# One step of a two-layer hybrid decoder on one core: the modulation units of the prelude in another order, and the first norm's last group in two halves

## The reference, cut to what matters

```python
def adaln(c, w, b):
    return jnp.split(jax.nn.silu(c) @ w + b, 6, axis=-1)

def modulate(x, g, shift, scale):
    return rms_norm(x, g) * (1.0 + scale[:, None, :]) + shift[:, None, :]
...
    for layer in range(DEPTH):
        mp = adaln(c_prompt, w_ada[layer], b_ada[layer])
        ...
        hp = modulate(yp, g_mix[layer], mp[0], mp[1])
        ...
            op, st_conv_p, st_gla_p = mix_ab(hp @ w_in_ab, conv0, gla0, ...)
```

## Time and profile before

| | |
|---|---|
| median of 3 runs | 2760.37 us |
| profiled execution, its own time | 2757.93 us |
| span of the profiled execution | 2756.2 us |
| PE busy | 2676.4 us, 97% of the span |
| DVE, ACT, POOL busy | 1426.5 us, 1160.5 us, 95.9 us |
| weights and inputs read | 592.02 MB |
| busy tenths of PE in the first two of 40 slices | 5, 8; 9 in nearly all others |

### The profile page before, as it was taken

One profiled execution on the slowest core, in us unless ns is written; L12 is line 12 of the kernel. 1 busy time (PEld: TensorE's weight loads), 2 busy tenths in 40 slices (PEclk: granted clock), 3 DMA queues, 4 the chain that ended last, 5 costly groups with the idle time before them and its releaser, 6 DMA issues.

```text
span 2756.2 us, 48520 instructions
## 1 busy us (share of the span) xinstructions
PE 2676.4 (97%) x20155; PEld 2473.9 (90%) x20155; DVE 1426.5 (52%) x1983; ACT 1160.5 (42%) x1521; POOL 95.9 (3%) x136
## 2 busy tenths in 40 slices
PE   5899999999999999999999999998999999999998
PEld 1688988888898888989999899898999999999998
DVE  1588967664444333444444556656445444445444
ACT  2433256453433322434443446535444433444433
POOL 1100011100000000000000000001000000000000
PEclk8999999999999999999999999999999999999999
DMA  9977769777777788776465544344544455445453
GB/s 392 370 286 275 288 231 179 295 281 284 272 290 260 292 318 317 281 282 244 160 237 161 163 153 136 110 134 159 168 162 161 147 160 190 158 164 167 143 161 128
DMA packets 110042, 603.61 MB, mean 219 GB/s; under 512 B 24829, under 2 KB 26301, under 8 KB 53578
## 3 DMA queue, kind: packets, MB, share of 16 engines
q1 hardware_dynamic: 109898, 601.56, 62.3%
HBM read 592.02 MB, written 9.49 MB: 218 GB/s over the span
## 4 chain that ended last, share of the span: by engine, by line
PE 91%; DMA 4%; DVE 2%; ACT 2%; issue 1%; SPq 0%; DVEq 0%; ACTq 0%
PE ps L882 27%; PE ps L884 26%; PE ps L883 26%; PE ps L1090 5%; DMA pre_ring<-in_w_ada 3%; DMA aring<-in_w_ada 1%; PE ps L1248 1%; ACT w_hi L1409 1%; PE ps L1249 1%; PE ps L1250 1%; PE ps L1103 1%; DMA raw<-in_w_dn 1%; DVE w_lo L1882 1%; PE ps L1072 0%; PE ps L1058 0%
## 5 line engine op out<-in xcount | busy, mean ns | idle before, releaser
L1882 DVE TENSOR_TENSOR w_lo<-raw,w_hi 128x2048 fp32r<-128x2048 f32 (+2 forms) x410 | 804.5, 1963 | 1024.7 <-ACT w_hi L1409 1024.6
L882 PE MATMUL ps<-act_hi,w_hi 128*128 128x288 f32 x4128 | 1234.1, 299 | 6.5 <-DVE w_lo L1882 4.6
L883 PE MATMUL ps<-act_hi,w_lo 128*128 128x288 f32 x4128 | 1219.7, 295 | 0.0
L884 PE MATMUL ps<-act_lo,w_hi 128*128 128x288 f32 x4128 | 1215.5, 294 | 0.0
L1409 ACT ACTIVATE w_hi<-raw 128x2048 fp32r<-128x2048 f32 (+2 forms) x410 | 673.9, 1644 | 1050.3 <-PE ps L884 1033.2
L882 PEld LDWEIGHTS ps<-act_hi,w_hi 128*128 128x128 f32 x4128 | 775.6, 188 | 58.6 <-issue 55.6
L884 PEld LDWEIGHTS ps<-act_lo,w_hi 128*128 128x128 f32 x4128 | 779.0, 189 | 0.0
L883 PEld LDWEIGHTS ps<-act_hi,w_lo 128*128 128x128 f32 x4128 | 777.1, 188 | 0.0
L882 PE MATMUL ps<-hid_hi,w_hi 128*128 128x288 f32 x1408 | 418.8, 297 | 0.6 <-DVE w_lo L1882 0.6
L883 PE MATMUL ps<-hid_hi,w_lo 128*128 128x288 f32 x1408 | 415.4, 295 | 0.0
L884 PE MATMUL ps<-hid_lo,w_hi 128*128 128x288 f32 x1408 | 414.0, 294 | 0.0
(11 more groups left out here) (339 smaller groups left out, 1757.6 us busy)
## 6 DMA issues: line engine op xcount, KB each, us to landing
raw<-in_w_gu SPq DMA_DIRECT2D x172, 1024.0 KB, 5.2
aring<-in_w_ada SPq DMA_DIRECT2D x166, 1024.0 KB, 6.9
raw<-in_w_dn SPq DMA_DIRECT2D x128, 704.0 KB, 4.1
raw<-in_w_ab SPq DMA_DIRECT2D x40, 1024.0 KB, 6.5
raw<-in_w_out SPq DMA_DIRECT2D x64, 512.0 KB, 4.7
raw<-in_w_cd SPq DMA_DIRECT2D x26, 1024.0 KB, 5.2
pre_ring<-in_w_ada SPq DMA_DIRECT2D x16, 1024.0 KB, 10.1
side<-in_w_ada SPq DMA_DIRECT2D x6, 1024.0 KB, 9.8
```

The source lines that it names most:

```text
L882: pe.matmul(bank, w_hi[:, h, cols], hi[:, kt, :], start=begin, stop=False)
L883: pe.matmul(bank, w_lo[:, h, cols], hi[:, kt, :], start=False, stop=False)
L884: mm = pe.matmul(bank, w_hi[:, h, cols], lo[:, kt, :], start=False, stop=end)
L1882: dve.tensor_tensor(w_lo[:, h, 0:w], raw[:, par, h * KT * P:h * KT * P + w], w_hi[:, h, 0:w].bitcast(F32), ALU.subtract).then_inc(split_do ...
```

## The change

The units are loaded and worked in the order 0, 4, 1, 5, 2, 6, 3, 7, so that shift and scale of a group of four tiles come one behind the other. All eight units are written out; the loops over units 1 to 3 are gone. `stat` comes after the third unit. `w_zr` and step 0's weights are loaded right after the third unit, too. `opening(0)` follows the turn of the fifth unit, `opening(1)` that of the sixth, `opening(2)` that of the seventh. The last group's norm, high part, low part and opening go in two halves of two tiles. No multiplication is added or left out.

```diff
+PRE_ORDER = [0, 4, 1, 5, 2, 6, 3, 7]
...
             def load_pre(u, s):
                 if not first_unit(u):
                     sp.wait_ge(ada_used, unit_no(u) * 4 + (s - 3))
-                rows = t["w_ada"][bass.ds(unit_no(u) * 4 + s, 1)]
-                sp.dma_start(pre_slot(s), rows.rearrange("a p n -> p (a n)")).then_inc(ring_landed[s], 16)
+                sp.dma_start(pre_slot(s), t["w_ada"][PRE_ORDER[unit_no(u)] * 4 + s]).then_inc(ring_landed[s], 16)
...
             sp.dma_start(x[:], t["xT"]).then_inc(x_landed, 16)
-            with sp.Fori(0, 3) as i:
-                for s in range(4):
-                    load_pre((i, 1), s)
-            sp.dma_start(raw[:, 1, 0:KT * P], t["w_zr"].rearrange("a p n -> p (a n)")).then_inc(zr_landed, 16)
-            for u in range(4, PRE):
+            for u in range(1, PRE):
                 for s in range(4):
                     load_pre((None, u), s)
-                if u == 4:
+                if u == 2:
+                    sp.dma_start(raw[:, 1, 0:KT * P], t["w_zr"].rearrange("a p n -> p (a n)")).then_inc(zr_landed, 16)
                     load_step(SEGS[0], 0, 0, 0)
...
-            stat()
-            for u in range(4, PRE):
+            for u in range(PRE):
                 for s in range(4):
                     ada_slot((None, u), s)
                 ada_turn((None, u))
-                if u > 4:
-                    opening(u - 5)
-            opening(3)
+                if u == 2:
+                    stat()
+                if u > 3:
+                    for k0, k1 in ((12, 14), (14, 16)) if u == PRE - 1 else ((4 * u - 16, 4 * u - 12),):
+                        opening(k0, k1)
...
                 for b in range(k1 - k0):
-                    j = k0 + b
+                    j = sets_of(k)[g][0] + b
                     ins = act.activation(tn[:, g % 2, b, 0:NP_TOK], tn[:, g % 2, b, 0:NP_TOK], ACT.Identity,
                                          scale=amod[:, j, 0:1], bias=mods[:, shift + j, 0:1])
+                    if k == 0 and g == 3 and b == 1:
+                        L.link(ins)
+                        act.wait_ge(tn_samples, set_no(k, g) + 1)
+                        act.activation(act_hi[:, k0:k0 + 2, :], tn[:, g % 2, 0:2], ACT.Copy).then_inc(nhi_done, 1)
+                        k0 += 2
...
-            squares_of_x(0)
-            squares_of_x(2)
-            with act.Fori(0, 3) as i:
-                ada_copy((i, 1))
-                squares_of_x(4 * i + 4)
-                squares_of_x(4 * i + 6)
+            for j in range(0, 6, 2):
+                squares_of_x(j)
+            ada_copy((None, 1))
+            for j in range(6, KT, 2):
+                squares_of_x(j)
+            ada_copy((None, 2))
             stat_rstd(D)
...
-            for g in range(4):
-                ada_copy((None, 4 + g))
-                norm_group(0, g)
-                if g == 0:
-                    split(SEGS[0], 0, 0, 0)
-                    split(SEGS[0], 0, 0, 1)
+            norm_group(0, 0)
+            ada_copy((None, 3))
+            split(SEGS[0], 0, 0, 0)
+            split(SEGS[0], 0, 0, 1)
+            norm_group(0, 1)
+            ada_copy((None, 4))
+            ada_copy((None, 5))
+            norm_group(0, 2)
+            ada_copy((None, 6))
+            ada_copy((None, 7))
+            norm_group(0, 3)
...
             for g in range(4):
-                ada_bias((None, 4 + g))
-                dve.wait_ge(ada_biased, 5 + g)
+                for u in (2 * g, 2 * g + 1):
+                    if u >= 3:
+                        ada_bias((None, u))
+                dve.wait_ge(ada_biased, 2 * g + 2)
                 scales(0, 4 * g, 4 * g + 4)
                 samples(0, g)
                 lo(0, g)
+                if g < 2:
+                    scaled(0, g + 2)
                 if g == 0:
                     split_lo(SEGS[0], 0, 0, 0)
                     split_lo(SEGS[0], 0, 0, 1)
-                if g < 2:
-                    scaled(0, g + 2)
```

More of the change, by code:

```diff
@@ L1191, in body, with opening @@
                         double_turn(p // 4)
-            def opening(g):
-                tiles_g = range(4 * g, 4 * g + 4)
+            def opening(k0, k1):
+                tiles_g = range(k0, k1)
                 def gate_half(h):
-                    if g == 0:
+                    if k0 == 0:
                         pe.wait_ge(split_done, h + 1)
@@ L1206, in gate_half @@
                         mm = pe.matmul(bank, w_hi[:, h, cols], act_lo[:, kt, :], start=False, stop=(kt == KT - 1))
-                    if g == 3:
+                    if k1 == KT:
                         mm.then_inc(half_done, 1)
-                pe.wait_ge(act_ready, 4 * g + 4)
+                pe.wait_ge(act_ready, k1)
                 gate_half(0)
-                if g == 0:
+                if k0 == 0:
                     pe.wait_ge(zr_split, 2)
@@ L1345, in _ @@
             pe.wait_ge(ones_set, 4)
-            for s in range(4):
-                ada_slot((None, 0), s)
-            ada_turn((None, 0))
-            with pe.Fori(0, 3) as i:
-                for s in range(4):
-                    ada_slot((i, 1), s)
-                ada_turn((i, 1))
-            stat()
-            for u in range(4, PRE):
+            for u in range(PRE):
                 for s in range(4):
@@ L1671, in norm_group @@
                 act.wait_ge(tn_samples, set_no(k, g) + 1)
-                act.activation(act_hi[:, k0:k1, :], tn[:, g % 2, 0:k1 - k0], ACT.Copy).then_inc(nhi_done, 1)
+                at0 = k0 - sets_of(k)[g][0]
+                act.activation(act_hi[:, k0:k1, :], tn[:, g % 2, at0:at0 + k1 - k0], ACT.Copy).then_inc(nhi_done, 1)
             def gate_terms(h):
@@ L2029, in ada_bias @@
                 dve.wait_ge(ada_cols, unit_no(u) + 1)
-                b = bass.ds(unit_no(u) * 4 + VEC["b_ada"], 4)
-                dve.tensor_tensor(mods[:, bass.ds(unit_no(u) * 4, 4), :],
+                at0 = PRE_ORDER[unit_no(u)] * 4
+                b = slice(at0 + VEC["b_ada"], at0 + VEC["b_ada"] + 4)
+                dve.tensor_tensor(mods[:, at0:at0 + 4, :],
                                   ps[:, SEL_BANK, 0:64].rearrange("p (q s) -> p q s", s=16)[:, :, 0:S9],
@@ L2166, in lo @@
                 k0, k1 = sets_of(k)[g]
-                dve.wait_ge(nhi_done, set_no(k, g) + 1)
-                js = slice(k0, k1)
-                dve.tensor_tensor(act_lo[:, js, :], tn[:, g % 2, 0:k1 - k0], act_hi[:, js, :].bitcast(F32), ALU.subtract) \
-                    .then_inc(act_ready, k1 - k0)
+                parts = [(k0, k0 + 2), (k0 + 2, k1)] if k == 0 and g == 3 else [(k0, k1)]
+                for n, (a0, a1) in enumerate(parts):
+                    dve.wait_ge(nhi_done, set_no(k, g) + 1 + n + (k > 0))
+                    js = slice(a0, a1)
+                    dve.tensor_tensor(act_lo[:, js, :], tn[:, g % 2, a0 - k0:a1 - k0], act_hi[:, js, :].bitcast(F32),
+                                      ALU.subtract).then_inc(act_ready, a1 - a0)
             def norm(k, final=False):
@@ L2487, in _ @@
                 dve.tensor_copy(sel2[rows, S9 * r:S9 * r + S9], sel[rows]).then_inc(sel2_ready, 1)
-            ada_bias((None, 0))
-            with dve.Fori(0, 3) as i:
-                ada_bias((i, 1))
+            for u in range(3):
+                ada_bias((None, u))
             for h in range(2):
```

2 lines of the change are left out of this document (1 added, 1 removed).

## The result

The changed kernel took 2766.2 us, the median of 8 runs (2765.3 to 2769.87), beside 2762.1 us for the kernel before (8 runs, 2759.13 to 2763.48). The medians are 4.1 us apart. The ratio on record is 1.0021, its 95% interval 1.0011 to 1.0031: slower by 0.2%, some 5.8 us by the ratio. The median lies above the range that was forecast.

The account below looks back on a forecast made before the run. PE was taken to bound the kernel, so only step 1's first matmul could move. Plus 0.2 us up to the eighth copy and minus 0.6 for the halves gave -0.4: 2757.5 us, 2760.0 on the median; range 2757.0 to 2765.0.

Parts of the forecast that it names:

- Bounds and the first part: PE bounds the kernel; early loads and squares are hidden by the stream; fifth unit's copy waits for split and group 1.
- The opening 4.95: Length in us forecast for `opening(0)` behind the fifth unit, taken from the kernel before's profile.
- Where `opening(0)` falls: Step placing `opening(0)` at 73.8 to 78.7 us, next load at 79.8, a dry spell of 2.8, seventh unit's end at 92.4.
- Of the 2.48 only 0.3 is left: Behind `opening(1)`, the eighth unit's load, issued 2.4 us early, loses 0.3 us of stream; bounds nothing and 2.48.
- Minus 0.6 us: Tail: halving the last group brings step 1's high part to 8.4 us behind the eighth unit's copy, from 9.02.
- the clock: Rival: PE runs `opening(0)`, perhaps also the last opening's halves, at 1.2 GHz, ending slower; chance 0.20.
- both places: Clock rival at `opening(0)` and the last opening's halves together: 2768.2 us; chance 0.05 of the 0.20.
- the first place: Clock rival at `opening(0)` alone: 2764.9 us at half the clock, 2762.5 if half of it is slow.
- Two dry spells: Rival: `opening(1)` also costs the load stream its full 2.48 us, 2.2 more than forecast: 2762.2 us; chance 0.08.
- Sum: Whole kernel: 0.2 - 0.6 = -0.4 us, 2757.5 for an execution like the profiled one, 2760.0 on the median; chance 0.60.

Follow-up runs that it names:

- `after_again`: The changed kernel, unaltered, run and profiled a second time; ratio to the kernel before 1.0019.
- `both_places`: The changed kernel plus matmuls with unread results behind slots of the fifth and seventh units, ahead of the last group's first half and behind its second; ratio 0.9999.
- `last_place`: The changed kernel plus matmuls with unread results only at the tail: six ahead of the last group's first half, three behind its second; ratio 1.0018.
- `w_all`: The changed kernel plus unread matmuls: two behind each fifth-unit slot, six ahead of the last group's first half, three behind its second; ratio 1.0012.
- `before_again`: The kernel before, unaltered, run and profiled a second time; ratio to its first measurement 0.9994.
- `spread`: The changed kernel with openings 0 to 2 in three pieces of 12 matmuls, behind the first three slots of the sixth to eighth units; ratio 1.0020.
- `unblocked`: The changed kernel with the split of step 0's weights ahead of group 0's norm on ACT and DVE; ratio to the kernel before 1.0005.

## Why the prediction was wrong

**Bounds and the first part: right.** The fifth unit's last slot starts at 70.01 (forecast 69.9), its copy at 71.85 (72.2), `opening(0)` at 73.93 (73.8). The copy is blocked by the split and group 1 as said.

**"The opening 4.95": wrong, and here the account breaks.** This is the step that failed: "Where `opening(0)` falls" took the length of the opening from a row at full clock, and here it ran at 1.2 GHz for the most part. From its start to the first slot behind it (81.45) it took 7.5 us. The load is issued at 82.58 in place of 79.8, so the seventh unit is that much later: 95.31 in place of 92.4.

**"Of the 2.48 only 0.3 is left": mis-sized.** The load is issued 2.5 us ahead of the seventh unit's last slot, as forecast, and the eighth unit's last slot comes 12.03 us later instead of 9.84: 2.2 us lost, near the outer bound of 2.48. In `after_again` the seventh and eighth copies are 10.89 apart, so it is some 1 us there, and 11.44 in `both_places`, 1.6 us, with `opening(0)` and `opening(1)` at full clock. So this term is too small without the slow clock, too: the forecast had 59.74 us from the third to the eighth copy (43.96 to 103.7), `both_places` took 60.95. In the changed kernel the stream does not stop there, it thins out (344 GB/s from 95 to 100 us, above); what makes the rest of the delay was not tried. The eighth copy there: 108.48 in place of 103.7.

**"Minus 0.6 us" for the halves: near in size, but only at a clock that the change took away.** At 2.4 GHz, in `both_places`, `last_place` and `w_all`, `w_hi` comes 8.54 us behind the copy, 0.5 less than before, with 0.68 and 0.76 us for the half instructions (forecast 0.6 and 0.7). The Trainium skill's fixed cost of a ScalarE instruction (VectorE: DVE Perf Modes, "The TRN2 errata"), from which the prediction worked out 0.67 and a gain of 0.54, was the better estimate: the row has 0.68, the gain was 0.5. In the changed kernel it is 10.19, and step 1's slow start costs another 1.4 us. The prediction noted that `opening(2)` had run in the gap of the tail for nothing; that it also kept PE's clock up there it did not see.

**The rivals.** The right one stood there, the clock, at 0.20 (0.05 for both places), with 2762.5 to 2764.9 for the first place and 2768.2 for both. Both happened, each for part of the stretch: 2766.2. What was set against it, that the later openings stand behind four slots in a row, is true of `opening(1)` and `opening(2)`, which ran at full clock, and says nothing of `opening(0)` and the last halves. It had the earlier trace rows for the case in question, PE at 0.50 while it worked on slots with gaps, and now put an opening right behind such slots. It also read that row too narrowly: the slow stretch did not end at 80 but at 82, 1.7 us ahead of the opening in place of 3.7, as finer windows of the kernel before show:

```profile
81.00:82.00 1.00, 1.00 (x8) 0.00 (x0) 0.00 (x0) 0.00 (x0) 0.00 (x0) 0.55 1.01 426
82.00:83.00 1.00, 0.28 (x6) 0.20 (x2) 0.00 (x0) 0.60 (x1) 0.00 (x0) 1.00 1.01 426
```

So in the old place the opening only just began at full clock, and in `before_again` it did not. "Two dry spells", at 0.08, came true in part as well, by the 1.0 to 2.2 us above. The rule of the Trainium skill that it named (TensorE: Matmul & The Clock Gate, "Part 1: The HAM clock gate"), that the throttled state is the default and activity releases it, agrees with the rows at 0.53 and 0.54 above, each behind waits. What the prediction drew from it, that spreading the matmuls between transfers is a loss, the runs do not show: in `spread` eight of the nine pieces between slots ran at full speed (12 matmuls in 1.57 us, a third of the 4.72 above).

**Sum.** Against the forecast the profiled first pair is late by 4.8 us at the eighth copy, 1.8 in the tail and 1.4 in step 1, 8.0 in all; its own time, 2766.03, lies 8.5 above the forecast of 2757.5 for such an execution. The kernel before's profiled execution was 4.2 us under its median of 2762.1, so the medians differ by less.

## What to carry to other kernels

Before moving matmuls to where their operands are first ready, look at the granted clock there: a stretch behind waits of one or two microseconds, here even of 0.7, can run at 1.2 GHz, and a matmul "for free" in a gap may be what keeps the next one at 2.4. The price multiplies where other work waits behind the slow stretch, as the loads did here. Here a group split in halves helped only where the engine that takes the halves was idle when the first one came; where it was not, the order of the matmuls inside decided who was released first.

## What was not expected

In the changed kernel's profile waits of 1.38 and 1.41 us, with 1.07 us of work between them, were followed by 1.2 GHz under an opening without gaps; and 1.2 GHz came there in all five runs of the new order that had `opening(0)` whole behind the fifth unit and no filler there (6.03 to 7.40 us). In `unblocked` the two waits were even shorter:

```profile
70.52 1.06 PE L1069 MATMUL ps<-pre_ring,cond 128*32 128x512 f32 x8 [0.68 <-DMA pre_ring<-in_w_ada]
...
72.30 1.30 PE L1110 MATMUL ps<-sel,adarow 128*128 128x9 f32 x8 [0.72 <-ACT adarow L1516]
73.45 0.59 PE L1201 MATMUL ps<-act_hi,w_hi 128*128 128x288 f32 x1
```

And the same program shows either level at the same place: in the kernel before `opening(0)` took 4.72 us in one profile and 6.06 in the other. Part of the spread between executions of one kernel may come from there; that is not shown.
